# Two-half scale and shift with three projection tiles in a mixer and expert kernel, and a shifted split of its expert tiles

## What is computed

```python
x = layer_norm(x, ln0_g, ln0_b)
mod = silu(c) @ ada_w + ada_b                  # 6 x 1024 values from one vector c
sh1, sc1, g1, sh2, sc2, g2 = split(mod, 6)
h = x * (1 + sc1) + sh1
z = h @ w_in                                   # 1024 x 1536: pool, recurrent, gate
y = concat(pool_mixer(z[:512]), conv + gated linear recurrence * gelu) @ w_out
x = layer_norm(ALPHA * x + g1 * y, ln1_g, ln1_b)
h = x * (1 + sc2) + sh2
# peer: per token and head the 16 best of 128 x 128 experts, softmax weights g over them
out = sum over picked experts e of g_e * gelu(h . u_e) * v_e
x = layer_norm(ALPHA * x + g2 * out, ln2_g, ln2_b)
```

## Time and profile before

| what | us |
|---|---|
| three runs: lowest, median, highest | 1495.73, 1501.62, 1505.71 |
| the profiled execution, its own time | 1495.95 |
| its span, first to last instruction | 1494.1 |
| around the span | 1.85 |
| TensorE busy, share of the span | 1437.9, 96% |
| VectorE busy, share of the span | 1246.9, 83% |
| ScalarE, GpSimd busy | 584.1, 526.0 |

### The profile page before, as it was taken

The page is one execution under the profiler, slowest core; times in us unless marked ns, Lnnn a source line. Parts: engine busy times, 40 slices in busy tenths (PEclk is TensorE's granted clock), DMA queues, the critical chain, the costliest instruction groups (busy, mean ns, idle before and its releaser), DMA issues.

```text
span 1494.1 us, 20739 instructions
## 1 busy us (share of the span) xinstructions
PE 1437.9 (96%) x7527; PEld 1242.8 (83%) x7527; DVE 1246.9 (83%) x2012; ACT 584.1 (39%) x689; POOL 526.0 (35%) x345
## 2 busy tenths in 40 slices
PE   8999999998999998888999999999999999999997
PEld 6775478898998888887888888888888888888886
DVE  7888969999999999568777777777877777777789
ACT  1461353333335888533333333333333333333331
POOL 0100225558554000036444444444444444444400
PEclk8999999999999999998999999999999999999999
DMA  9824440024646698999999999999999999999961
GB/s 384 298 113 169 153 175 1 1 92 141 225 166 210 210 291 255 332 340 404 386 341 345 342 338 339 348 341 334 344 346 340 340 336 346 341 343 336 344 223 58
DMA packets 158892, 402.30 MB, mean 269 GB/s; under 512 B 11344, under 2 KB 79056, under 8 KB 156144
## 3 DMA queue, kind: packets, MB, share of 16 engines
q1 hardware_dynamic: 120256, 262.17, 51.1%
q0 software_dynamic: 38288, 139.08, 24.4%
q10 hardware_dynamic: 288, 0.29, 0.1%
HBM read 359.56 MB, written 41.94 MB: 269 GB/s over the span
## 4 chain that ended last, share of the span: by engine, by line
PE 62%; DVE 29%; ACT 3%; DMA 3%; issue 2%; SPq 0%; DVEq 0%; ACTq 0%
PE bank L949 19%; PE bank L948 19%; PE bank L947 19%; DVE arena L1545 2%; DVE arena L1537 2%; DVE arena L1274 1%; DVE arena L1587 1%; DVE arena L1542 1%; DVE arena L1534 1%; DVE u_lo L1634 1%; DVE arena L1641 1%; DVE arena L1583 1%; DMA early_dram<-arena 1%; DVE arena L1539 1%; DVE arena L1586 1%
## 5 line engine op out<-in xcount | busy, mean ns | idle before, releaser
L947 PE MATMUL bank<-h_hi,u_hi 128*128 128x384 f32 (+1 forms) x1256 | 441.7, 352 | 16.9 <-DVE u_lo L1634 9.0
L948 PE MATMUL bank<-h_lo,u_hi 128*128 128x384 f32 (+1 forms) x1256 | 434.8, 346 | 0.0
L949 PE MATMUL bank<-h_hi,u_lo 128*128 128x384 f32 (+1 forms) x1256 | 434.3, 346 | 0.0
L947 PE MATMUL bank<-v_hi,w_hi 128*128 128x512 f32 x744 | 291.2, 391 | 7.0 <-DVE w_lo L1683 7.0
L949 PE MATMUL bank<-v_hi,w_lo 128*128 128x512 f32 x744 | 296.1, 398 | 0.0
L948 PE MATMUL bank<-v_lo,w_hi 128*128 128x512 f32 x744 | 292.5, 393 | 0.0
L1677 DVE TENSOR_TENSOR v_lo<-v_raw,v_hi 128x2048 fp32r<-128x2048 f32 x62 | 142.1, 2292 | 157.7 <-ACT v_hi L838 157.7
L947 PEld LDWEIGHTS bank<-h_hi,u_hi 128*128 128x128 f32 x1256 | 237.0, 189 | 35.7 <-POOL u_lo L586 10.3
L948 PEld LDWEIGHTS bank<-h_lo,u_hi 128*128 128x128 f32 x1256 | 237.2, 189 | 12.3 <-issue 0.7
L949 PEld LDWEIGHTS bank<-h_hi,u_lo 128*128 128x128 f32 x1256 | 237.0, 189 | 9.4
L838 ACT ACTIVATE v_hi<-v_raw 128x2048 fp32r<-128x2048 f32 x62 | 118.8, 1917 | 314.0 <-PE bank L949 289.2
(11 more groups left out here) (240 smaller groups left out, 1834.2 us busy)
## 6 DMA issues: line engine op xcount, KB each, us to landing
u_raw<-ut_dram SPq DMA_DIRECT2D x128, 512.0 KB
v_raw<-v_dram SPq DMA_DIRECT2D x64, 1024.0 KB, 7.1
gate_in<-gates_dram SPq DMA_DIRECT2D x64, 384.0 KB
wbuf<-ada_w_dram SPq DMA_DIRECT2D x9, 2048.0 KB, 13.2
early_dram<-arena SPq DMA_DIRECT2D x64, 192.0 KB
gates_dram<-wbuf SPq DMA_DIRECT2D x3, 4096.0 KB, 16.4
w_raw<-early_dram SPq DMA_DIRECT2D x64, 192.0 KB
wbuf<-wq_dram SPq DMA_DIRECT2D x4, 2048.0 KB, 7.8
```

The lines of the kernel that those rows point to most:

```text
L947: pe.matmul(out, a_hi, b_hi, start=(k == 0), stop=False)
L948: pe.matmul(out, a_hi, b_lo, start=False, stop=False)
L949: return pe.matmul(out, a_lo, b_hi, start=False, stop=(k == n - 1))
```

## The change

**Front.** The pieces come in the order shift 0, scale 0, shift 1, scale 1 (`COLUMNS`), and scale and shift are made in two halves of 4 chunks (`first_scales`). VectorE takes (4, 4, 5, 5) products of a piece and TensorE the other (4, 4, 3, 3). The weights of tiles 0 to 3 have buffers of their own and come behind the second piece. VectorE makes only `nmean`, and ScalarE normalises x and writes both "hi" and full h of all chunks. TensorE sums chunks 0 to 3 of three tiles, then the modulation of the second half, then chunks 4 to 7. Two of the `spare` runs (2 and 6 matmuls) go. Tile 3 keeps `u_hi[1]` and is split by ScalarE when tile 1 is summed. Pieces 4 and 5 are summed behind tile 5, and the decay chain stands in VectorE's stream behind piece 5.

**Expert tiles.** `T_SCATTER` goes from 16 to 20 and `T_STORE` from 12 to 8. Piece 11 is loaded ahead of the stretch, v and gates earlier in it. No `picks` come before the first pair; from pair 12 to 27 there are five to a pair instead of four. The order of a pair's 36 matmuls over its two experts changes, and at the end one gating of v rows goes ahead of the last regular preparation.

```diff
-    (("win", 1), 0), (("win", 0), 1), (("ada", 4), 2), (("ada", 5), 3), (("win", 2), 2), (("ada", 6), 3),
+    (("win", 0), 1), (("ada", 4), 2), (("ada", 5), 3), (("win", 2), 2), (("ada", 6), 3),
-BY_VECTOR = (6, 6, 6, 5)
+BY_VECTOR = (4, 4, 5, 5)
+COLUMNS = (0, 2, 1, 3) + tuple(range(4, 12))
-SPARE_FIRST, SPARE_ADA, SPARE_Z, SPARE_Q = 12, 2, 6, 5
+SPARE_FIRST, SPARE_ADA, SPARE_Q = 12, 2, 5
+FIRST_TILES = 3
-U_EARLY = PICKS - SLOT_PAIRS * (PER * AT_GELU + 1)
+EXTRA_FROM = PER * AT_GELU - (PICKS - SLOT_PAIRS * PER * AT_GELU)
-T_TURN, T_RANK, T_SCATTER, T_STORE = 35, 36, 16, 12
+T_TURN, T_RANK, T_SCATTER, T_STORE = 35, 36, 20, 8
-BANKS_X = (2, 3, 4, 5, 6)
+BANKS_X = ((3, 4, 5, 6), (2, 3, 4, 5, 6))
-LATE_ADA_AT = 1
-FIRST_V = 5
+FIRST_V = 2
-FIRST_HI = T_STORE - 4
-AT_GATE2 = 6
+FIRST_HI = T_STORE - 2
+AT_GATE2 = T_STORE - 1
...
+                if (name, j) == ("ada", 1):
+                    sp.dma_start(first_in, w_in[1][:, :, 0:2 * P]).then_inc(s_first, 16)
+                    sp.dma_start(third_in, w_in[1][:, :, 2 * P:3 * P]).then_inc(s_in3, 16)
+                    sp.dma_start(fourth_in, w_in[1][:, :, 3 * P:]).then_inc(s_in4, 16)
...
+            sp.wait_ge(s_scmm, 4 + SD // 4)
+            sp.dma_start(late_ada[1], ada_w[11]).then_inc(s_late[1], 16)
             for s in range(T_STORE):
...
-                if s == LATE_ADA_AT:
-                    sp.wait_ge(s_scmm, 4 + SD // 4)
-                    sp.dma_start(late_ada[1], ada_w[11]).then_inc(s_late[1], 16)
...
+            for tb in range(TB):
+                act.wait_ge(s_nmean, tb + 1)
+                act.activation(xt[:, tb, :], xt[:, tb, :], ACT.Identity, bias=nmean[:, tb:tb + 1],
+                               scale=rstd[:, tb:tb + 1]).then_inc(s_ln0, 1)
+            act.wait_ge(s_zero, 4)
             hi_weights(0)
+            modulate(0, scale1, bias1, range(0, 1))
             hi_weights(1)
-            modulate(0, BANKS_X, scale1, bias1)
             hi_weights(2)
-            act.wait_ge(s_zero, 4)
+            modulate(0, scale1, bias1, range(1, 4))
+            modulate(0, scale1, bias1, range(4, KD))
...
+            for k in range(KD // 2):
+                pe.wait_ge(s_hlo, k + 1)
+                for n in range(FIRST_TILES):
+                    pe.wait_ge(s_wtlo, n + 1)
+                    z_chunk(n, k)
+            pe.wait_ge(s_sc, 1)
+            upper_modulation(2)
+            modulation(2)
+            transposes(0, range(KD // 2, KD))
+            upper_modulation(3)
+            modulation(3)
+            for k in range(KD // 2, KD):
                 pe.wait_ge(s_hlo, k + 1)
                 z_chunk(0, k)
                 z_chunk(1, k)
+            for k in range(KD // 2, KD):
+                z_chunk(2, k)
...
-            z_tiles(2, 5)
+            z_tiles(FIRST_TILES, 6)
             modulation(4)
             modulation(5)
-            z_tiles(5, 6)
...
-                for j in range(2):
-                    w_of, v_of = pair_of(c % 2, j)
-                    for t in range(DENSE):
-                        for half in range(2):
+                for t in range(DENSE):
+                    for half in range(2):
+                        for j in range(2):
+                            w_of, v_of = pair_of(c % 2, j)
                             mm = values(w_of, v_of, t, half, isinstance(i, int) and i + c + j == 0, False)
...
+            for half in range(2):
+                for j in (2 * half, 2 * half + 1):
+                    partial_modulation(j, range(BY_VECTOR[j]))
+                if half == 0:
+                    low_weights_of(0)
+                first_scales(half)
+                for k in range(4 * half, 4 * half + 4):
+                    low_input(0, scale1, bias1, range(k, k + 1))
+                    if k in (0, 1):
+                        low_weights_of(k + 1)
+            low_weights_of(3)
             partial_modulation(4)
...
-            low_weights_of(3)
             low_weights_of(4)
             partial_modulation(5)
+            decay_terms(0)
+            decay_terms(1)
             convolve((0, 1))
             low_weights_of(5)
...
-                picks(one)
+                picks(2 if EXTRA_FROM <= c < AT_GELU * PER else 1)
                 lo_w(c + 1)
```

More of the change, by code:

```diff
@@ L926, in upper_modulation, with transposes @@
                     for k in range(BY_VECTOR[j], KD):
-                        pe.matmul(bank[7][:, 4 * j + m:4 * j + m + 1], piece("ada", j)[:, k, m * P:(m + 1) * P],
+                        at = 4 * COLUMNS[j] + m
+                        pe.matmul(bank[7][:, at:at + 1], piece("ada", j)[:, k, m * P:(m + 1) * P],
                                   silu_c[:, k:k + 1], start=(k == BY_VECTOR[j]), stop=(k == KD - 1))
-            def transposes(stage_of, banks, chunks=range(KD)):
-                base = KD * stage_of
-                pe.wait_ge(s_ln, TB * (stage_of + 1))
+            def transposes(stage_of, chunks=range(KD)):
+                base, banks = KD * stage_of, BANKS_X[stage_of]
+                pe.wait_ge(s_ln if stage_of else s_ln0, TB)
                 for k in chunks:
                     if stage_of and k == KD // 2:
-                        pe.wait_ge(s_ln, 2 * TB + 1)
+                        pe.wait_ge(s_ln, TB + 1)
                     if k >= len(banks):
@@ L954, in _ @@
             upper_modulation(0)
-            transposes(0, BANKS_X, range(len(BANKS_X)))
+            transposes(0, range(KD // 2))
             modulation(0)
@@ L973, in z_chunk @@
                     mm.then_inc(s_zmm, 1)
-            pe.wait_ge(s_wtlo, 2)
-            for k in range(KD):
-                if k + len(BANKS_X) < KD:
-                    transposes(0, BANKS_X, range(k + len(BANKS_X), k + len(BANKS_X) + 1))
+            for k in range(KD // 2):
[10 more added lines that the diff above has]
+            for k in range(KD // 2, KD):
                 pe.wait_ge(s_hlo, k + 1)
@@ L1052, in _ @@
             spare(SPARE_Q, 1)
-            transposes(1, BANKS_X, range(len(BANKS_X)))
+            ahead = len(BANKS_X[1])
+            transposes(1, range(ahead))
             pe.wait_ge(s_yres, 2 * TB)
@@ L1063, in _ @@
             for k in range(KD):
-                if k + len(BANKS_X) < KD:
-                    transposes(1, BANKS_X, range(k + len(BANKS_X), k + len(BANKS_X) + 1))
+                if k + ahead < KD:
+                    transposes(1, range(k + ahead, k + ahead + 1))
                 pe.wait_ge(s_hlo, KD + k + 1)
@@ L1706, in picks, with prepare @@
                 done[0] += count
-            def prepare(c, count=SLOT_PAIRS):
-                one = count // 4
+            def prepare(c):
                 if c == AT_GELU * PER:
```

143 lines of the change are left out of this document (72 added, 71 removed).

## The result

The changed kernel takes 1509.54 us (median of 8 runs, 1508.21 to 1519.88) against 1499.13 for the kernel before (8 runs): ratio 1.0085, 95% interval 1.0056 to 1.0113, so 8 to 17 us slower. The forecast was 1499, no change; the interval excludes that. The profiled execution is 1519.88, one of two of the eight near 1519; the other six took 1508 to 1511.

A forecast was written before the change was run, and what follows sets the result against it. TensorE, busy 96% of the span, was taken to bound the kernel, with VectorE pacing the scatter. Front +24.5, scatter and store -26.5, pairs +1, end -1 sum to -2: 1499 us, no change; own range 1491 to 1508, outer 1480 to 1517.

The forecast's parts named there:

- The forecast's own sign of being wrong: Tile 6 before 100, the scatter stretch longer than 148, or TensorE idle in pairs 12 to 27.
- Scatter, the failed step: Scatter with four more tiles: TensorE's own work 137.1 plus 4 idle, 141 us; bounds 137 and 150.6.
- Store stretch: Behind the scatter to the first values: both large waits go, transfers set 54 us (51 to 61).
- Tail in all: Scatter plus store stretch to the first values: 195 us after 221.5, so -26.5 (best 188, worst 211.6).
- Front: From the start to tile 6: it starts at 112.6 instead of 88.06, +24.5 us (+16.5 to +30.5).
- The chain of VectorE's order: Front, behind tile 1: VectorE's work in its order ends with tile 5's low part 24 us after tile 1.
- The clock term (+8): Front: longer one-column runs and fewer spares lower TensorE's clock, +8 us (up to 14), tile 1 at 71.
- this passes through whole: Tile 6 to the scatter: same order, TensorE waits little, so the front's +24.5 us arrives undiminished.
- Pairs and end: Pairs 12 to 27 with a fifth pick: +1 us, up to 8; gating at the end: -1 (0 to -2).
- The stand at tile 5 costs nothing: Front rival: with a warm front and VectorE's later chain setting tile 6, 12 us come back: 1480; chance 0.16.
- The clock stays up in the front: Front rival: no clock loss, so +16.5 - 26.5 = -10, 1492; chance 0.20.
- The scatter gives nothing back: Scatter rival: jitter keeps all 13.5 us idle, store backlog makes first gates 7 late: +14.5, 1516; chance 0.18.

The follow-up runs named there:

- Each part alone: Kernel before with only the expert-tile (tail) part of the change: 1491.38 us; kernel before with only the front part: 1519.78 us.
- tail_phase: Kernel before with the expert-tile part alone, VectorE's low parts in the scatter placed by 2 step + 2 instead of 2 step + 3: 1474.77 us.
- after_phase: Changed kernel with one number changed, VectorE's low parts in the scatter placed by 2 step + 2 instead of 2 step + 3: 1496.02 us.
- after_order: Changed kernel, VectorE making piece 4 before tile 3's low part and tile 5's low part before decay and convolution: 1505.97 us.
- tail_split: Kernel before with the expert-tile part alone, each 4 MB gate store in the scatter issued as four of 1 MB: 1494.41 us.
- after_byvec: Changed kernel with the products of the four pieces shared as before (VectorE 6, 6, 6, 5; TensorE the rest): 1500.93 us.

## Why the prediction was wrong

It lost 14.7 us on the sum (-2 against +12.7); changing the one number of the rule gives 14.0 of them back. Each part alone, the front came 4.1 cheaper than forecast and the tail gave 21.1 less. The forecast's own sign of being wrong, a scatter longer than 148 us, is what came.

- **Scatter, the failed step.** "I take 137.1 + 4 idle = 141 (bounds: no idle 137, all 13.5 idle kept 150.6)", against 133.9 before, so +7; measured +23.7. (The table's marks lie 4.8 further apart, so its 162.5 stands against a forecast of 146 and an upper bound of 155.4.) TensorE's own work was right: by the table's marks 124.2 + 4 x 4.16 = 140.9, and tail_phase has 141.0. The term that failed is TensorE's idle time: 4 forecast, 18.3 measured, of which three waits of 4.5 are the low parts of tiles 7, 12 and 17. Busy times of TensorE and VectorE were put side by side, and the bound of "all idle kept" took the idle time of the old order for the worst case, but the new count of tiles made a new order. With the rule mended 3.8 are idle and the stretch takes 144.8, +6.1: the forecast.
- **Store stretch**: 54 forecast, 56.0 measured by the table's marks (54.7 in tail_phase) and some 3 more by the forecast's own, which begin earlier: within its bounds, but the gain is 28.5 and not 33.6. The reasons hold: picks and piece 11 were the two waits, and the runs price them at 11.2 and 3.6. One wait of 4.4 for `u_lo` is left where the forecast had none over 4.
- **Tail in all**: -26.5 forecast; -5.4 alone, -24.1 with the mended rule.
- **Front**: +24.5 forecast (16.5 to 30.5), +20.4 alone, and +30.4 at tile 6 in the profiled execution. First product 33.4 forecast, 38.12 measured; tile 1 summed at 71, measured 77.8, by the cold bound of 77; the low part of tile 5 24 us behind that, measured 101.78 - 77.8 = 24.0; wait at tile 5 8 to 11, measured 8.66; from its start to tile 6 5.4 + 2 + 8.8 + 1.4 = 17.6 forecast, 118.49 - 101.84 = 16.7 measured. The chain of VectorE's order was right to the us. The clock term (+8) was too small for this execution, where 63 at full clock became 77.8. In the profiled execution of after_phase, whose front is the same, tile 5 starts at 92.17, which puts the sum of tile 1 near 68: there +5 would have done. The +8 lies between the two.
- **"this passes through whole"**: 28.4 of 30.4 reach the scatter. But TensorE's stand at tile 5 seems to be worth only half its length: after_order took it away and got 3.9 of 8.66, with overlapping intervals.
- **Pairs and end**: +1 and -1 forecast, +0.4 in all; TensorE is busy 60.60 of 60.60 us behind the first values, and 210.00 of 210.00 from 860 to 1070, where the pairs with five picks lie. The picks cost nothing there. They are sixteen, one in each of pairs 12 to 27, and not the twelve of the prediction.
- **Rivals.** "The stand at tile 5 costs nothing" (1480): no. "The clock stays up in the front" (1492): no, 0.62 to 0.67 from 17.5 to 80, and 0.73 from 30 to 60 in after_phase's profiled execution. "The scatter gives nothing back" (1516) named the right stretch and came nearer to 1509.5 than the forecast, but by another mechanism: jitter and the backlog of stores. tail_split shows that the stores did not do it, and tail_phase that full engines did not. Its chance of 0.18 was too small for a step in which two engines that are busy 97% and 93% of it (141.01 and 135.33 of 144.80 in tail_phase) were interleaved by a rule whose places for 20 tiles the prediction had not worked out.
- **The clock.** The Trainium skill, "TensorE: Matmul & The Clock Gate", section "HAM oscillation", blames idle gaps. In the front the trace shows what that rule does not cover: 0.62 with 12.50 of 12.50 busy in one-column products and transposes, 0.87 for the same stream in another execution, and 0.90 with 9.27 of 12.50 busy in after_byvec. In the scatter it agrees: with the long waits gone the clock is 0.99 instead of 0.94.

Still open: why executions of one front differ in the clock, and what of the front's 20.4 us is the clock and what the count of products.
